# Block 1 of a four-layer network on one core: the order of VectorE's work in three heads, and x's first rows loaded by halves

## The reference

```python
h = rmsnorm(x, norm_g)
proj = jnp.einsum('bsd,dc->bsc', h, w_in)
aq, ak, av, az, buv, bz, cq, ck, cv, cz, gl = split_cols(proj)
...
oa = diff_attention(qa, ka, va, lam)          # 4 heads, two softmaxes each, rotated q and k
ya = rmsnorm(oa, subln_g) * (1 - lam_init) * silu(az)
...                                           # yb: gelu, layernorm, a mix over 128 tokens
...                                           # yc: dilated windows, 8 heads of 64, times silu(cz)
gates = jax.nn.sigmoid(gl.reshape(B, S, N_BRANCH, D))
merged = jnp.einsum('bsnd,nbsd->bsd', gates, pb)
return x + jnp.einsum('bsd,de->bse', merged, w_out)
```

## Time and profile before

| | |
|---|---|
| median of three runs | 2322.68 us (2322.1 to 2323.67) |
| the profiled execution | 2325.3 us, its span 2323.5 us |
| busy: TensorE | 2308.4 us, 99% |
| busy: VectorE | 1481.2 us, 64% |
| busy: ScalarE | 978.6 us, 42% |
| granted clock of TensorE | 0.999 over the span |

### The profile page before, as it was taken

How to read it: one execution, slowest core, us unless ns; L and a number is a source line. 1 busy time by engine, 2 the same in 40 slices (tenths; PEclk the granted TensorE clock), 3 DMA queues, 4 the chain that set the end, 5 groups by cost and what they waited for, 6 DMA issues and landing times.

```text
span 2323.5 us, 30126 instructions
## 1 busy us (share of the span) xinstructions
PE 2308.4 (99%) x11442; PEld 1881.9 (81%) x11442; DVE 1481.2 (64%) x2781; ACT 978.6 (42%) x1811; POOL 0.2 (0%) x4
## 2 busy tenths in 40 slices
PE   9999999999999999999999999999999999999998
PEld 6888888888888878888877788888887768888887
DVE  6788763435478784444587668566567777658565
ACT  5356542223446553222567543232336764323222
POOL 0000000000000000000000000000000000000000
PEclk9999999999999999999999999999999999999999
DMA  4333334333243333233221133314313112422322
GB/s 167 107 105 105 104 96 112 92 99 100 84 117 109 97 103 114 93 100 117 65 88 55 56 127 102 127 55 145 118 37 97 55 46 100 145 82 91 127 64 99
DMA packets 74766, 226.84 MB, mean 98 GB/s; under 512 B 15296, under 2 KB 16192, under 8 KB 73856
## 3 DMA queue, kind: packets, MB, share of 16 engines
q1 hardware_dynamic: 74336, 224.14, 30.9%
q10 hardware_dynamic: 288, 0.79, 0.1%
HBM read 205.36 MB, written 2.10 MB: 89 GB/s over the span
## 4 chain that ended last, share of the span: by engine, by line
PE 96%; DVE 2%; ACT 1%; issue 0%; DMA 0%; DVEq 0%; SPq 0%
PE bank L590 25%; PE bank L592 25%; PE bank L591 25%; PE bank L2235 2%; PE bank L2237 2%; PE bank L2236 2%; PE bank L1310 2%; PE bank L2054 1%; PE bank L2013 1%; PE bank L1294 1%; PE bank L2038 1%; PE bank L524 1%; PE bank L1283 1%; PE bank L1281 1%; PE bank L2067 1%; PE bank L2096 0%
## 5 line engine op out<-in xcount | busy, mean ns | idle before, releaser
L590 PE MATMUL bank<-h_hi,w_hi 128*128 128x512 f32 x1984 | 784.7, 396 | 0.7 <-DVE sz L1769 0.3
L592 PE MATMUL bank<-h_lo,w_hi 128*128 128x512 f32 x1984 | 773.4, 390 | 0.0
L591 PE MATMUL bank<-h_hi,w_lo 128*128 128x512 f32 x1984 | 773.0, 390 | 0.0
L1157 DVE TENSOR_TENSOR w_lo<-raw_w,w_hi 128x1024 fp32r<-128x1024 f32 x314 | 378.9, 1221 | 97.4 <-ACT w_hi L1145 94.1
L590 PEld LDWEIGHTS bank<-h_hi,w_hi 128*128 128x128 f32 x1984 | 372.7, 188 | 82.5 <-issue 8.3
L592 PEld LDWEIGHTS bank<-h_lo,w_hi 128*128 128x128 f32 x1984 | 372.4, 188 | 79.8
L591 PEld LDWEIGHTS bank<-h_hi,w_lo 128*128 128x128 f32 x1984 | 372.9, 188 | 72.1
L1145 ACT ACTIVATE w_hi<-raw_w 128x1024 fp32r<-128x1024 f32 x314 | 327.6, 1054 | 159.5 <-DMA raw_w<-w_dram 159.1
L2472 ACT ACTIVATE nrm<-bank 128x512 f32<-128x512 f32 x44 | 26.4, 599 | 288.4 <-PE bank L592 288.4
L1611 ACT ACTIVATE ext<-bank 128x512 f32<-128x512 f32 x48 | 28.7, 598 | 274.3 <-PE bank L592 274.3
L1918 DVE TENSOR_TENSOR rope_a<-ext,bank 128x512 f32<-128x512 f32 x32 | 22.0, 688 | 165.8 <-PE bank L592 109.7
(11 more groups left out here) (372 smaller groups left out, 3504.6 us busy)
## 6 DMA issues: line engine op xcount, KB each, us to landing
raw_w<-w_dram SPq DMA_DIRECT2D x312, 512.0 KB, 3.6
down_raw<-w_dram SPq DMA_DIRECT2D x36, 512.0 KB, 4.5
extra_raw<-w_dram SPq DMA_DIRECT2D x10, 512.0 KB, 4.6
k_lo<-k_lo SPq DMA_DIRECT2D x32, 128.0 KB, 2.3
ln_row<-row_dram SPq DMA_DIRECT2D x4, 1024.0 KB, 6.6
last_raw<-w_dram SPq DMA_DIRECT2D x8, 512.0 KB, 4.6
rowp<-row_dram SPq DMA_DIRECT2D x2, 1024.0 KB, 11.9
rot_t<-raw_t SPq DMA_DIRECT2D x128, 16.0 KB
```

The lines of the kernel that those rows point to most:

```text
L590: nc.tensor.matmul(dst, lh, rh, start=start, stop=False)
L591: nc.tensor.matmul(dst, ll, rh, start=False, stop=False)
L592: return nc.tensor.matmul(dst, lh, rl, start=False, stop=stop)
L1157: nc.vector.tensor_tensor(lo_of(u), raw_of(u), hi_of(u).bitcast(F32), ALU.subtract) \
```

## The change

At the start, x's first block is loaded in two parts: rows 0 to 63 on ScalarE's queue as before, rows 64 to 127 on SyncE's queue behind `const` and `colp` and ahead of the first weights. The first block's semaphore now counts both. In block 1, at step 2 of heads 4 to 6, VectorE does the epilogue (heads 5 and 6) and the normalisation ahead of the rotation of the next head's keys.

```diff
             for tb in range(NB):
-                if tb:
-                    sp.dma_start(x[:, tb, :], x_in[tb * P:(tb + 1) * P, :]).then_inc(x_loaded[tb], 16)
+                rows = slice(0 if tb else HD, P)
+                sp.dma_start(x[rows, tb, :], x_in[tb * P:(tb + 1) * P, :][rows, :]).then_inc(x_loaded[tb], 16)
...
             if layer == 0:
-                act.dma_start(x[:, 0, :], x_in[0:P, :]).then_inc(x_loaded[0], 16)
+                act.dma_start(x[0:HD, 0, :], x_in[0:HD, :]).then_inc(x_loaded[0], 16)
...
-                act.wait_ge(x_loaded[tb], 16)
+                act.wait_ge(x_loaded[tb], 16 if tb else 32)
...
-                    if second1(a, qb):
+                    if qb == 2 and a in JOINED1 and a > N_A:
+                        dve.wait_ge(y_ready, at(y_ready, 3 + a))
+                        epilogue(a - 1, False)
+                    if qb in (1, 2) and a in JOINED1:
                         normalise(a, qb)
                     if before in ROTATE1:
                         rotate(*ROTATE1[before])
...
-                    elif qb == (2 if a in JOINED1 else 1) and a > N_A:
+                    elif qb == 1 and a > N_A and a not in JOINED1:
                         epilogue(a - 1, False)
...
-                    if not second1(a, qb):
+                    if qb not in (1, 2) or a not in JOINED1:
                         normalise(a, qb)
```

## The result

The changed kernel takes 2326.9 us (median of 20 runs, 2324.67 to 2328.9), the kernel before, run beside it on the same chip, 2323.03 (20 runs, 2321.45 to 2325.13). The ratio is 1.0015 with a 95% interval of 1.0009 to 1.002, which is 3.5 us more (2.1 to 4.6); the two medians as they stand differ by 3.9. That is "the same" by the bound of 0.2% and inside the range given, 1.8 us above the predicted time; the direction, slower, is outside the uncertainty of the measurement. The profiled execution took 2326.11 us, with a span of 2324.3.

The account below looks back on a forecast made before the run. TensorE, busy 99% of the span, bounds the kernel, so only its idle time counts. Front −0.4 and two layers +2.8 us on the 2322.68 median give 2325.1 us, range 2322.3 to 2327.0, chance 0.89 within.

Parts of the forecast that it names:

- Head 5: saved and spent again: Head 5, third step: 1.5 us of waits at L1310 and L1294 go, return ahead of L1281; net +0.25 us.
- Head 6: VectorE queued behind a product: Head 6, third step: VectorE idles 2.1 us ahead of the epilogue, keys 3.95 us late, TensorE 1.4 us behind.
- Head 4: hidden: Head 4, third step: VectorE idles some 2.3 us, head 5's keys come about 3.3 us later; costs nothing.
- The placements' landing: Keys' placements at heads 5 and 6: the last lands 2.3 us after its issue.
- Rival (c): Placements on the path land slower than 2.3 us, making the kernel slower by over 0.2%; chance 0.08.
- (a): Waits at L1310 and L1294 go and nothing comes back, the keys' delay hidden: 2319.3 us; chance 0.08.
- (b): Head 5 as forecast, but head 6 hides its wait: 2322.8 us; chance 0.17.
- The front: the term that was mis-sized: Start: const and colp share DMA engines with 256 KB of x instead of 512 KB; −0.4 us.
- the slip of up to 2 us "without harm": Start: x's first block may land 2 us later at no cost; at 3 us about 1 would show.
- My cover of 2.3 us: Start: ScalarE had x's root mean square at 6.39, 2.3 us before VectorE's L553 used it.
- Its other citation: Skill's DMA port swizzle: partitions 0 to 63 reach half the DMA ports, so the front gives nothing; sum 2325.5.
- The sum: Whole kernel: front −0.4, each layer +1.4, twice +2.8; +2.4 us on 2322.68 gives 2325.1 us.

Follow-up runs that it names:

- head 5 alone: VectorE's new order in head 5's third step only, heads 4 and 6 and the front as in the kernel before: 2324.43 us, ratio 1.0.
- the heads alone: VectorE's new order in heads 4 to 6, x's first block loaded whole as in the kernel before: 2326.78 us, ratio 1.0013.
- head 6 alone: VectorE's new order in head 6's third step only, heads 4 and 5 and the front as in the kernel before: 2325.64 us, ratio 1.0007.
- kernel before again: The unchanged kernel before, profiled a second time to see whether its start repeats: 2324.29 us.
- split last: Kernel before with the split of a weight (L1157) moved behind the normalisation in head 5's third step: 2322.09 us, ratio 0.9989.
- changed kernel again: The changed kernel, nothing further edited, profiled a second time: 2325.39 us.
- front alone: Kernel before with only x's first block loaded in halves on two queues, VectorE's old order in the heads: 2323.45 us, ratio 0.9999.
- version that beats both: Kernel before with head 6's queries rotated before head 5's second-step weight split, x's first block whole on SyncE's queue behind const and colp: 2318.96 us, ratio 0.9975.

## Why the prediction was right, step by step

- **Head 5: saved and spent again.** Right. Both waits went, one of 1.52 us came back at L1281 (forecast 1.8); net +0.16 us (forecast +0.25). The kernel with head 5 alone shows the same.
- **Head 6: VectorE queued behind a product.** Right, place and size: idle 1.90 us (forecast 2.1), the keys 3.7 us late (3.95), wait at L1281 1.04 us (1.1), TensorE 1.23 us behind at that point (1.15), and about 0.1 us more behind it, which the prediction had named and not counted. Lengthening the delay lengthened the wait one for one, which shows that the keys set that start.
- **Head 4: hidden.** Right: idle 2.31 us (2.3), and nobody waits.
- **The placements' landing.** Right: 2.3 us, longest 2.4, in both heads, though now on the path. Rival (c), 2325.1 and up through slow landings, did not happen; nor did (a) or (b), whose signs (no wait at L1281 near 285, or near 312) are absent.
- **The front: the term that was mis-sized.** Forecast −0.4 us. L1173 moved by 0.32, 0 and 0.19 us in the three profiles with the halves, and x, which landed for a read at 4.78 before, was read at 5.87, 6.54 and 7.02: the slip of up to 2 us "without harm" was used up. My cover of 2.3 us for it came from one profile in which TensorE's four products took 3.75 us, because the clock rose only at 12.03; where they took 1.95, TensorE waited 0.37 and 1.05 us for the normed x (L524). Timed alone the front is −0.3 us and can't be told from nothing. The halves brought x later than the whole, and not only because the second is issued later: 256 KB issued at 1.63 on SyncE's queue, with the other half under way, were read at 5.87 to 7.02, and the whole 512 KB issued there at 1.64, in the last kernel, at 5.56. That halves bring nothing agrees with the Trainium skill's DMA: Bandwidth & Descriptors (Rules for kernel authors), by which two transfers to disjoint halves of the partitions serialize and aren't worth the bother. The prediction had named that rule and given x's lateness no price. Its other citation, by which the front gives nothing at all, is as well borne out as the 0.4 us: the timed difference has room for both.
- **The sum.** +3.5 us (2.1 to 4.6) measured against +2.4 forecast, which lies in the interval. The heads, 2.8 in the forecast, are 3.0 in the profiles and 3.0 timed alone. The rest, 0.5 us of the 3.5, is inside the interval and isn't resolved.

What stays open: what the front's halves cost or give on average. The spread between executions of one kernel at that place is larger than the effect. Pairs of profiles in which the clock rose at nearly the same moment (the table below) say that it depends on that moment. With an early rise the halves are late: L524 starts at 9.07 and 9.56, against 8.56 with x whole, and at 265 us they are 1.0 and 0.5 us behind. With a rise at 9.9 they are ahead: 10.37 against 10.56 with the heads alone, and at 265 us 0.9 us ahead of it (0.2 ahead of head 6 alone, whose clock rose at 9.46). These are single profiles, so this is a reading and not shown.

## What to carry to other kernels

When a step is moved ahead in an engine that works in order, cost it by what it waits for and by what stands behind it with the least spare time: here a 1.8 us block was moved ahead of the keys, and at head 6 its wait for a product made that 3.7 us. Waits at the end of a backlog are better cured where the backlog begins: filling VectorE's known idle stretch, fifteen microseconds upstream, gave 3.2 us, where trading places downstream lost 3. To bring a small constant sooner, take the large load from in front of it instead of halving it; that halved `colp`'s landing (3.8 to 1.9 us) and made x 0.8 us late (4.78 to 5.56) instead of 1.1 to 2.2.

## What the runs showed of the hardware

**The clock rises at a different moment in each execution.** In the first microseconds each pass of TensorE over 512 columns, in float32, starts 0.85 us behind the one before it, and later 0.43 us (for the two passes at L1195, 1.92 against 1.02 us in two profiles of one kernel). It is tempting to say that the granted clock has nothing to do with this, since the windows' row over the slow passes of the kernel before reads 1.00:
```profile
8.00:10.00 2.00, 2.00 (x3) 0.74 (x3) 1.97 (x3) 0.00 (x0) 0.00 (x0) 1.00 1.01 410
```
That 1.00 is no measurement. Each trace holds a list of the stretches for which the clock was recorded, and the row counts time that no entry covers as full clock. In this trace the list begins at 12.03 us, with the upper level (1.00, that is 2.4 GHz), and its passes go over to the short time at 12.0. So it is in all fourteen profiles: every pass that ended before the first entry is a long one, every pass that started behind it a short one. Their ratio, 0.85 to 0.43, is that of the two levels. Some of them:

| profile | first entry of the clock's list, us | L524 starts, us | shift at 265 us |
|---|---|---|---|
| kernel before | 12.03 | 11.14 | 0.0 |
| kernel before again | 8.93 | 10.05 | −1.7 |
| heads alone | 9.82 | 10.56 | −1.3 |
| split last | 4.43 | 8.56 | −3.4 |
| changed kernel | 9.91 | 10.37 | −2.2 |
| changed kernel again | 4.39 | 9.56 | −2.9 |
| front alone | 4.82 | 9.07 | −2.4 |
| version that beats both | 6.28 | 8.10 | −3.7 |

All that follows shifts with it. At 265 us, before any edit in the heads has moved TensorE, the ten profiles of kernels whose start is that of before had shifts from 0.0 to −3.4 us, and the earlier the first entry, the further ahead they were, with two exceptions of a few tenths; the three with x in halves (−2.2, −2.4, −2.9) lie among them. So a single pair of profiles tells nothing about an edit at the start, unless the clock rose at the same moment in both. I argue, and did not show, that this is also most of the spread of 4 us among the timed runs.

**Long waits lowered the clock, but not each time.** Behind the waits of 1.0 to 1.6 us at L1281 the granted clock stayed at 1.00. Behind the 2.63 us at L1281 it was 0.50, that is 1.2 GHz: by the trace's list from 312.60, just before the wait ended, to 319.42, and from 868.97 to 875.79 in the second layer. The 0.82 of the row above is a mean over both levels. Behind the 2.74 us at L1310 it was 0.50 from 310.63, one microsecond after the wait, to 314.04 (in the rows below 0.53, again a mean over both levels):
```profile
305.00:309.00 4.00, 1.84 (x9) 1.17 (x7) 3.83 (x9) 0.87 (x2) 0.00 (x0) 1.00 0.00 0
310.50:313.00 2.50, 2.35 (x11) 2.36 (x12) 2.36 (x7) 1.53 (x5) 0.00 (x0) 0.53 0.92 184
```
In the second layer of that same kernel TensorE waited 2.75 us at L1310, to 865.06, and the clock stayed at 1.00. So of four waits of 2.6 to 2.8 us three were followed by the lower level. In the first case it added 3.0 us a layer to a wait of 2.6, more than the wait itself; in the second 1.2 us, in one layer. The changed kernel did not come to this.
